# Encoder layer, feed-forward stage: other places for the next block's input norms and turns, and another wait ahead of the first FF1 product

## What is computed

```python
y = jnp.concatenate([rms_norm(ya, g_out_a[i]), rms_norm(yb, g_out_b[i])], axis=-1)
y = jnp.einsum('bse,ed->bsd', y, w_out[i])
h = h + rms_norm(y, g_attn_post[i])
xn = rms_norm(h, g_mlp_pre[i])
f = jnp.square(jax.nn.relu(jnp.einsum('bsd,df->bsf', xn, w_ff1[i])))      # D_FF = 4096
f = jnp.einsum('bsf,fd->bsd', f, w_ff2[i])
h = h + rms_norm(f, g_mlp_post[i])
gate = jax.nn.sigmoid(jnp.einsum('bsd,de->bse', rms_norm(h, g_ple[i]), w_ple_gate[i]))
h = h + gate * jnp.einsum('bsp,pd->bsd', p[i], w_ple_proj[i])
```

## Time and profile before

| | us |
|---|---|
| median of three runs | 3700.36 |
| the profiled execution | 3707.64 |
| its span in the profile | 3705.8 |
| PE busy | 3484.8 (94%) |
| DVE / ACT / POOL busy | 2387.2 / 1891.5 / 1870.5 |
| mean granted TensorE clock | 0.970 of full speed |

### The profile page before, as it was taken

One profiled execution on the slowest core, in us unless ns is written; L12 is line 12 of the kernel. 1 busy time (PEld: TensorE's weight loads), 2 busy tenths in 40 slices (PEclk: granted clock), 3 DMA queues, 4 the chain that ended last, 5 costly groups with the idle time before them and its releaser, 6 DMA issues.

```text
span 3705.8 us, 56160 instructions
## 1 busy us (share of the span) xinstructions
PE 3484.8 (94%) x18428; PEld 2953.7 (80%) x18428; DVE 2387.2 (64%) x4351; ACT 1891.5 (51%) x3554; POOL 1870.5 (50%) x1188
## 2 busy tenths in 40 slices
PE   7999979999999999999689998999999999899997
PEld 6878768888888889999578877788777887778885
DVE  5434558888888878778365566555565556655554
ACT  2222258888888777778343354333443344433342
POOL 4545512332000133434457766677675776757773
PEclk9999989999999999999789999999999999999998
DMA  4444334443002144343224444344443443434441
GB/s 163 160 168 156 124 106 145 153 152 130 17 17 51 24 89 89 63 86 106 90 91 153 143 135 154 120 153 148 133 162 109 152 150 136 166 107 143 150 151 57
DMA packets 288913, 444.97 MB, mean 120 GB/s; under 512 B 175189, under 2 KB 194077, under 8 KB 282685
## 3 DMA queue, kind: packets, MB, share of 16 engines
q1 hardware_dynamic: 279356, 428.51, 37.1%
q10 hardware_dynamic: 9344, 13.73, 1.0%
HBM read 377.92 MB, written 76.71 MB: 123 GB/s over the span
## 4 chain that ended last, share of the span: by engine, by line
PE 40%; DVE 7%; ACT 2%; issue 1%; DMA 1%; POOL 0%; SPq 0%; DVEq 0%; ACTq 0%
PE feed_bank L1618 39%; DVE feed_total L1923 2%; DVE feed_res L1926 1%; DVE feed_xn L1899 1%; DVE feed_xT L1908 1%; PE feed_bank L1609 1%; DMA feed_w_raw<-w_ff_dram 0%; DVE feed_total L1983 0%; POOL feed_w_split L1569 0%; DMA feed_w_raw<-scr_wT 0%; DVE feed_ms L1887 0%; ACT feed_w_split L1804 0%; DVE feed_sums L2029 0%; ACT feed_xT L1776 0%; DVE feed_rec L1890 0%
## 5 line engine op out<-in xcount | busy, mean ns | idle before, releaser
L1569 POOL TENSOR_TENSOR feed_w_split<-feed_w_raw,feed_w_split 128x1024 fp32r<-128x1024 f32 x424 | 1071.0, 2534 | 295.6 <-ACT feed_w_split L1804 276.7
L1618 PE MATMUL feed_bank<-feed_w_split,feed_comb 128*128 128x512 f32 x3648 | 864.5, 397 | 48.5 <-POOL feed_w_split L1569 17.8
L1618 PEld LDWEIGHTS feed_bank<-feed_w_split,feed_comb 128*128 128x128 f32 x3648 | 695.3, 192 | 206.2 <-POOL feed_w_split L1569 26.1
L1618 PE MATMUL feed_bank<-feed_xT,feed_w_split 128*128 128x512 f32 x3072 | 702.6, 390 | 7.9 <-DVE feed_total L2034 5.4
L1618 PEld LDWEIGHTS feed_bank<-feed_xT,feed_w_split 128*128 128x128 f32 x3072 | 578.8, 189 | 129.8 <-issue 6.6
L358 PE MATMUL proj_bank<-proj_w_split,proj_xT 128*128 128x512 f32 (+1 forms) x1920 | 413.3, 376 | 18.7 <-ACT proj_st L426 16.1
L358 PEld LDWEIGHTS proj_bank<-proj_w_split,proj_xT 128*128 128x128 f32 x1920 | 340.0, 193 | 87.3 <-ACT proj_st L426 20.6
L930 DVE TENSOR_TENSOR mixa_pT<-mixa_turned,mixa_pT 128x512 fp32r<-128x512 f32 x512 | 348.2, 685 | 81.3 <-ACT mixa_pT L876 77.6
L1566 POOL TENSOR_SCALAR feed_w_split<-feed_w_raw 128x1024 fp32r<-128x1024 f32 x200 | 227.4, 1137 | 341.3 <-issue 311.1
L876 ACT ACTIVATE mixa_pT<-mixa_turned 128x512 fp32r<-128x512 f32 x512 | 307.2, 600 | 148.8 <-PE mixa_turned L819 129.7
L777 PE MATMUL mixa_out_acc<-mixa_pT,mixa_v_hl 128*128 128x512 f32 x1028 | 365.8, 437 | 0.5 <-DVE mixa_pT L930 0.5
(11 more groups left out here) (191 smaller groups left out, 5137.8 us busy)
## 6 DMA issues: line engine op xcount, KB each, us to landing
feed_w_raw<-w_tail_dram SPq DMA_DIRECT2D x200, 512.0 KB, 3.7
feed_w_raw<-scr_wT SPq DMA_DIRECT2D x160, 512.0 KB, 3.3
proj_w_raw<-w_in_dram SPq DMA_DIRECT2D x39, 1024.0 KB, 5.0
feed_w_raw<-w_ff_dram SPq DMA_DIRECT2D x64, 512.0 KB, 3.6
scr_table<-scr_bias SPq DMA_DIRECT2D x8, 1520.0 KB, 9.0
proj_x_t<-x_dram SPq DMA_DIRECT2D x20, 512.0 KB, 6.0
mixa_q_in<-scr_qA SPq DMA_DIRECT2D x36, 256.0 KB, 3.4
mixb_q_in<-scr_qB SPq DMA_DIRECT2D x18, 512.0 KB, 5.9
```

The source lines that it names most:

```text
L1569: pool.tensor_tensor(w_sp[1][:, slot, :], w_raw[:, slot, :], w_sp[0][:, slot, :].bitcast(F32), ALU.subtract).then_inc(w_lo, 1)
L1618: mm = pe.matmul(dst, lhs, rhs, start=start, stop=stop)
```

## The change

The diff, whole but for context. It moves the requests, norms and turns to other chunk positions; it requests `p` after chunk 87 and not after chunk 84; and it makes the first two FF1 products of a block wait for the count of `prod_done` (the DVE products that read the two PSUM banks) and not for all additions of the block before (`o_done`). `prod_done` starts at 2, so every other wait on it is written 2 higher.

```diff
-    LOAD_Y = {44: 0, 56: 1, 66: 2, 81: 3}
-    NORM_Y = {50: 0, 60: 1, 77: 2, 80: 3}
-    TURN_Y = {74: 0, 76: 1, 80: 2, 83: 3}
+    LOAD_Y = {40: 0, 48: 1, 58: 2, 83: 3}
+    NORM_Y = {40: 0, 48: 1, 75: 2, 79: 3}
+    TURN_Y = {73: 0, 76: 1, 79: 2, 82: 3}
...
-    P_LOAD, P_AT = 84, 87
+    P_LOAD, P_AT = 87, 87
...
             pool.sem_inc(o_done, 2)
+            pool.sem_inc(prod_done, 2)
...
                     if g == 0 and j < 2:
-                        pe.wait_ge(o_done, b * 8 + 2)
+                        pe.wait_ge(prod_done, b * 8 + j + 1)
...
                         elif n == 1:
-                            pe.wait_ge(prod_done, b * 8 + (t + 3))
+                            pe.wait_ge(prod_done, b * 8 + (t + 5))
                     elif kind == "ple":
                         if not (n == 0 and t < 2):
-                            pe.wait_ge(prod_done, b * 8 + (4 * n + t - 1))
+                            pe.wait_ge(prod_done, b * 8 + (4 * n + t + 1))
...
                         if n == 1:
-                            act.wait_ge(prod_done, b * 8 + (t + 1))
+                            act.wait_ge(prod_done, b * 8 + (t + 3))
...
-                        ve.wait_ge(prod_done, b * 8 + (q + 1))
+                        ve.wait_ge(prod_done, b * 8 + (q + 3))
```

## The result

| | before | changed |
|---|---|---|
| median of four runs, us | 3704.25 (3699.84 to 3708.99) | 3672.77 (3670.11 to 3678.97) |
| span of the profiled execution, us | 3705.8 | 3667.2 |
| start of the first FF1 product, us | 1872.5 | 1868.2 |
| from there to the end, us | 1833.3 | 1799.0 |

The ratio is 0.9908, with a 95% interval of 0.989 to 0.9927: some 27 to 41 us faster. The prediction was 3665.4, with a range of 3656 to 3686. The span says 38.6 us, but 4.3 of these lie ahead of the first FF1 product, in stages that the change doesn't touch; the stage of the change gained 34.3 us.

A forecast was written before the change was run, and what follows sets the result against it. PE, busy 94% of the span, was taken as the bound, so only its gaps and slow matmuls could be gained. 9.8 + 19.8 + 5.4 = 35.0 us off the median 3700.4 gave 3665.4 us, range 3656 to 3686.

The forecast's parts named there:

- The sum: Whole stage: gains of 9.8, 19.8 and 5.4 us add to 35.0 us, taken off the median 3700.4.
- Group 2: Group 2's "m" stretches: norms 0 and 1 moved to chunks 40 and 48 remove the gap; 9.8 us, bounds 0 and 9.8.
- Group 3: Group 3's "m" chunks and turns: SP's two stops ahead of weights go; 19.8 us, bounds 8.7 and 23.7.
- The hand-made timetable of ACT: Group 3, block 0, followed from its start: chunk 79 comes 0.3 us late, chunk 83 1.0 us late.
- The first FF1 product: Start of FF1: PE's 1.81 us wait for the last addition goes three times; 5.4 us, bounds 0 and 7.1.
- The bound of 7.1: FF1 wait's upper gain, 7.1 us, if slow matmuls behind one gap go too (45.37 us where 43.7 is usual).
- G1 and G3 should keep their lengths: Stages G1 and G3: no change expected; growth, by low halves meeting DVE's residual chain in another phase, would refute the prediction.
- (a): Group 3: ACT takes SP's place, most stalls stay at chunks 79 and 83; gain 23.9, 3676.5 us; chance 0.17.
- (b): Group 2: norm 1 under "f" chunks hands the same lateness on; gain 25.2, 3675.2 us; chance 0.06.
- (c): FF1: something other than the additions, such as weights, holds PE; gain 29.6, 3670.8 us; chance 0.05.
- (d): (a), (b) and (c) together: gain 8.7, 3691.7 us, within 0.3% of no change; chance 0.06.
- (e): Slower: ACT's stops precede high halves, chunks 74 to 83; decides above 12 us extra stalls a block; 3727 us; chance 0.04.

The follow-up runs named there:

- e7: The changed kernel with norm 1 at chunk 50 in place of 48; group 2 120.4 us (changed 116.0), to the end 1802.1 us (changed 1799.0).
- e5: The kernel before with only y tile 3 requested after chunk 83 and p after 87; group 3 125.2 us (before 148.3), to the end 1809.6 us.
- e8: e4 with y tile 3 requested after chunk 82 in place of 83; ratio to before 0.9886, median 3667.38 us.
- e1: The kernel before with only the changed wait of the first two FF1 products; to the end 1823.1 us (before 1833.3).
- e3: The kernel before with only group 3's new requests, norms and turns; group 3 127.8 us (before 148.3), to the end 1823.0 us.
- e2: The kernel before with only tiles 0 and 1 requested and normalised at chunks 40 and 48; group 2 116.0 us (before 125.7), to the end 1825.6.
- e6: The kernel before with only norms 2 and 3 and the four turns earlier; group 3 128.2 us (before 148.3), to the end 1816.2 us.
- e4: The changed kernel with p split at chunk 86 in place of 87; ratio to before 0.9887, median 3665.76 us.
- e10: e4 with norms and turns of before, and G1's high halves made by ACT in place of POOL; ratio to before 0.9854, median 3651.77 us.

## Why the prediction was right, step by step

**The sum.** 35.0 us were forecast for the stage, 34.3 were measured there. The median gave 31.5, with 27 to 41 in its interval; the difference to the forecast of 3665.4 is 7.4 us, of which 3.9 is that the median of before itself moved from 3700.36 to 3704.25 with one more run. The kernel's three other stages vary by some us from run to run (the first FF1 product starts between 1868.2 and 1878.7 us in the twelve profiles), so no total of a single run could have tested the sum.

**Group 2, 9.8 us: measured 9.7.** The size was right because it came from stretches with their slow matmuls; the gaps alone would have given 6.5. The cause was right in both its parts, the squares and the table load, which were counted at 1.3 us each; in the gap the norm's place weighs twice the table load (e7). Norm 1 at chunk 48 met POOL just as norm 0 had at 50 (one sum of 2.62 us on DVE at 2070.13), and chunk 50 took up the lateness, as the step said.

**Group 3, 19.8 us: measured 20.5.** SP's two stops and the weights behind them were the cause (e5). The hand-made timetable of ACT gave 0.3 us at chunk 79 and 1.0 at chunk 83; measured are 0 and 0.6. The 1.0 came from two sources, the landing of tile 3 and the mean on DVE, 1.31 us where I had taken 1.6; of these only the mean bounds (e8). What the step did not see is that the norms and turns need not have moved: with them in place the stretch is 0.9 us shorter (e5). It costed the change as a whole and never the halves.

**The first FF1 product, 5.4 us: measured 5.5 (e1).** The gap of 1.81 is gone in each block. The bound of 7.1, by slow matmuls that go with it, was reached in block 1, in e1 and in the changed kernel as well, where 192 matmuls take 43.7 us in place of 45.4. The wait can't be credited with that part: in e5 the gap of 1.81 us still stands ahead of block 1's FF1, and the 192 matmuls take 43.8 us there too.

**What failed: "G1 and G3 should keep their lengths".** They should have lost the 5.4 us of the FF1 gap and nothing else; they lost 2.0, so 3.4 were given back there. The text named the place and the kind ("meet there in another phase") among what would make it wrong, but put no price on it and no term into the range. In the gaps ahead of the first turn and behind it, the kernel before had 15.7 us in three blocks and the changed kernel 20.4; other gaps and slow matmuls took back part of the 4.7. A price could have been estimated from the rows: a DVE instruction that finds POOL at a low half may wait up to one of these, 2.41 us, and 1.7 was measured (2.94 for 1.22). What failed is thus the overlap of DVE's chain with POOL, a term put at nothing.

That the sum came out 0.7 us too high and not 3.4 is luck. Slow matmuls gone at FF1, for which the forecast had taken none (1.7 us), 0.7 more in group 3 and some tenths elsewhere made up for most of the loss, and they have nothing to do with it.

**Rivals.** (a), (b) and (c) are out by e3, e2 and e1, and (d), which is all three, with them. (e) had its mechanism, ACT in front of the high halves, at work with 0.6 us a block, a twentieth of its point of decision.

The rule cited from the Trainium skill (SBUF — State Buffer, Who interferes with whom) had more to say than I took from it. It states that the shared ports are held "for the whole instruction" and by whoever comes first; by that, a small shift is enough to swap the two engines. The trace agrees: 0.7 us of shift, and 1.22 and 2.94 us for the same DVE instruction. For `tensor_scalar` it agrees with the 2.32 us of e8. The prediction put the price of that under group 3 at some 2 us; the gaps ahead of chunk 83 sum to 1.9.

## What to carry to other kernels

When an in-order DMA queue waits for a compute step, look first at what stands behind that wait: moving the request behind the urgent ones (e5) was worth as much there as making the step earlier (e6), and needs no other order on the engines. Where DVE and GpSimd both work from SBUF, look at which instruction of DVE waits behind which of GpSimd's. In this kernel a pair of additions that needs 2.5 us alone took 5.3 beside GpSimd. Moving one instruction out of the chain passed part of its wait on to the next (e4: 6.3 us to the end, of the 9 to 11 hoped for); taking work off GpSimd in that stretch gave more (e10: 12.9 us). Count a removed gap with the half-clock matmuls behind it, and compare stages, not totals, when other stages vary by as much as the gain.

## What the runs showed of the hardware that I had not expected

Which of DVE and POOL waits hangs on tenths of a microsecond: with DVE 0.17 us ahead, DVE takes 1.22 us and POOL 3.31; with POOL 0.54 us ahead, DVE takes 2.94 and POOL 2.39. And removing the one does not remove the wait: it passes on to the next instruction of DVE, with 3.30 us for 1.44.

A mean over 128 x 2 numbers can take 2.32 us, and here the shape decides. In the profiles of the kernel before, of the changed kernel and of e8, each of the 24 means over 128 x 2 that began inside a low half of POOL took 1.03 to 2.36 us, and the 24 others 0.15 to 0.17. The means over 128 x 1, at the same line, took 0.13 to 0.16 us, beside POOL or not. One that ran inside a low half of the usual length, in the kernel before (POOL's row, then DVE's):

```profile
2272.78 2.40 POOL L1569 TENSOR_TENSOR feed_w_split<-feed_w_raw,feed_w_split 128x1024 fp32r<-128x1024 f32 x1
...
2274.18 0.15 DVE L1887 TENSOR_SCALAR feed_ms<-feed_ssq 128x1 f32<-128x1 f32 x1 [0.89 <-ACT feed_junk L1751]
```

So two means of one column each might escape the wait that holds chunk 83; no run tried it.
